# Encoder block on one core: eleven attention tiles are transposed in 32-by-32 blocks by VectorE and put in place by DMA, and six weight strips get their low halves from GpSimd

## The reference, cut to what matters

```python
def axial_gqa_attention(q, k, v, q_g, k_g):
    q = rms_norm(q.reshape(bsz, seq, A_Q_HEADS, HEAD_DIM), q_g)
    k = rms_norm(k.reshape(bsz, seq, A_KV_HEADS, HEAD_DIM), k_g)
    ...
    def block(s0):
        qb = lax.dynamic_slice_in_dim(q, s0, Q_BLOCK, axis=1)
        s = jnp.einsum('bqkgd,bskd->bkgqs', qb, k).astype(jnp.float32)
        p = jax.nn.softmax(s, axis=-1).astype(v.dtype)
        return jnp.einsum('bkgqs,bskd->bqkgd', p, v)
```

## Time and profile before

| what | us |
|---|---|
| median of 3 runs | 862.43 (862.28 to 864.42) |
| the profiled execution | 861.86 |
| its span in the profile | 859.8 |
| TensorE busy in the span | 839.4 (98%) |
| VectorE busy | 379.3 (44%) |
| ScalarE busy | 264.1 (31%) |
| GpSimd busy | 29.0 (3%) |

### The profile page before, as it was taken

One profiled execution on the slowest core, in us unless ns is written; L12 is line 12 of the kernel. 1 busy time (PEld: TensorE's weight loads), 2 busy tenths in 40 slices (PEclk: granted clock), 3 DMA queues, 4 the chain that ended last, 5 costly groups with the idle time before them and its releaser, 6 DMA issues.

```text
span 859.8 us, 10399 instructions
## 1 busy us (share of the span) xinstructions
PE 839.4 (98%) x4197; PEld 513.2 (60%) x4197; DVE 379.3 (44%) x665; ACT 264.1 (31%) x461; POOL 29.0 (3%) x50
## 2 busy tenths in 40 slices
PE   9999999999999999999999999999999998989996
PEld 8898866687878888888534343344433433334343
DVE  6377987797715254427322237223131321321351
ACT  6333876695624233216011010010100101001231
POOL 1050000000000000003000000000000000000010
PEclk9999999999999999999999999999999999999999
DMA  9830112023034234884899999999999999999996
GB/s 285 179 98 2 50 50 98 25 76 109 20 123 143 84 107 144 311 356 180 331 410 425 429 428 426 429 428 427 428 428 427 426 430 428 426 423 429 427 420 265
DMA packets 81490, 239.19 MB, mean 278 GB/s; under 512 B 8102, under 2 KB 63526, under 8 KB 65828
## 3 DMA queue, kind: packets, MB, share of 16 engines
q1 hardware_dynamic: 76016, 235.94, 69.7%
q10 hardware_dynamic: 5284, 2.09, 1.0%
q0 software_dynamic: 144, 0.51, 0.1%
HBM read 235.92 MB, written 2.62 MB: 277 GB/s over the span
## 4 chain that ended last, share of the span: by engine, by line
PE 88%; DMA 8%; DVE 1%; ACT 1%; issue 1%; POOLq 0%; POOL 0%; SPq 0%; DVEq 0%; ACTq 0%
PE psum L1657 21%; PE psum L1169 11%; PE psum L1689 11%; PE psum L1171 11%; PE psum L1170 11%; DMA wslot<-in_w_down 7%; PE psum L1614 3%; PE psum L1708 3%; PE psum L1357 2%; PE psum L1818 2%; PE psum L1326 2%; PE psum L1369 1%; PE psum L1669 1%; PE psum L1175 1%; PE psum L1622 1%; PE psum L1379 1%
## 5 line engine op out<-in xcount | busy, mean ns | idle before, releaser
L1657 PE MATMUL psum<-wslot,xinT 128*64 128x512 f32 x1000 | 221.9, 595 | 3.7 <-DMA wslot<-in_w_up 1.9
L1657 PEld LDWEIGHTS psum<-wslot,xinT 128*64 128x64 f32 x1000 | 69.5, 137 | 141.3 <-issue 131.8
L1689 PE MATMUL psum<-wslot,actT 128*64 128x512 f32 x424 | 95.8, 596 | 4.5 <-DMA wslot<-in_w_down 4.5
L1169 PE MATMUL psum<-hT_hi,w_hi 128*128 128x512 f32 x208 | 82.4, 396 | 0.9 <-DVE oT_lo L1991 0.9
L1170 PE MATMUL psum<-hT_lo,w_hi 128*128 128x512 f32 x208 | 81.2, 390 | 0.0
L1171 PE MATMUL psum<-hT_hi,w_lo 128*128 128x512 f32 x208 | 81.2, 390 | 0.0
L1892 DVE TENSOR_TENSOR w_lo<-w_raw,w_hi 128x1024 fp32r<-128x1024 f32 (+1 forms) x46 | 52.9, 1174 | 44.4 <-ACT w_hi L805 44.3
L1689 PEld LDWEIGHTS psum<-wslot,actT 128*64 128x64 f32 x424 | 29.4, 137 | 60.4 <-issue 58.0
L1101 ACT ACTIVATE actT<-psum 128x512 f32<-128x512 f32 x16 | 9.6, 597 | 171.2 <-PE psum L1669 171.2
L2305 DVE TENSOR_TENSOR x<-x,psum 128x512 f32<-128x512 f32 x48 | 29.7, 681 | 57.0 <-PE psum L1708 57.0
L2295 DVE TENSOR_TENSOR y_lo<-psum,y_hi 64x512 fp32r<-64x512 f32 x28 | 19.3, 689 | 80.4 <-ACT y_hi L1111 80.0
(11 more groups left out here) (285 smaller groups left out, 1306.5 us busy)
## 6 DMA issues: line engine op xcount, KB each, us to landing
wslot<-in_w_up SPq DMA_DIRECT2D x24, 2048.0 KB, 25.0
wslot<-in_w_gate SPq DMA_DIRECT2D x24, 2048.0 KB, 23.9
wslot<-in_w_down SPq DMA_DIRECT2D x22, 2048.0 KB, 22.4
w_raw<-in_w_in SPq DMA_DIRECT2D x34, 512.0 KB, 4.7
wslot<-in_w_up SPq DMA_DIRECT2D x15, 1024.0 KB, 11.0
wslot<-in_w_down SPq DMA_DIRECT2D x15, 1024.0 KB, 27.5
wslot<-in_w_gate SPq DMA_DIRECT2D x14, 1024.0 KB, 11.2
w_raw<-in_w_out SPq DMA_DIRECT2D x8, 512.0 KB, 4.9
```

Source lines behind the costliest of these rows:

```text
L1169: pe.matmul(out_, s_hi, m_hi, start=(k == 0), stop=False)
L1657: mm = pe.matmul(bank[2 * e + n][CAP * f:CAP * f + CAP, :], xinT[:, HALF * h + k, CAP * e:CAP * e + CAP], wslot[place_of(m)][:, k % PART, ...
L1689: mm = pe.matmul(bank[4 + e][CAP * f:CAP * f + CAP, :], actT[:, e, k, CAP * h:CAP * h + CAP], wslot[place_of(m)][:, k % PART, SEQ * f:SEQ ...
```

## The change

In the even heads (0, 2, 4, 6) the tiles 0, 1 and 2 (in head 6 only 0 and 1) no longer go over TensorE: eleven tiles of 32. For those the steps are:

- VectorE only makes the reciprocal; ScalarE multiplies the tile (`scale_probs`), ahead of which TensorE's transposes, and after which `read_probs`, are gone.
- VectorE transposes all 32x32 blocks of the tile with one instruction into a new buffer `blocks` (`turn_blocks`), one unit after the reciprocal.
- SP copies `blocks` into `pT` with 16 DMAs of 32 partitions for each of the four heads (`move_blocks`), ahead of the loads of strips 18, 21, 23 and 24.
- `pT` and `oT` get another order of tokens, which ScalarE and VectorE undo when they read the result of `values_a`. `values_a` now also waits for `blocks_in` and stands in units 10, 18 and 26.

The low halves of strips 14 to 19 move from VectorE to GpSimd. The `far` copy of mixer B moves from ahead of its first unit to ahead of its second.

The core of the diff:

```diff
+        def block_tiles(h):
+            return NT - 2 if h == A_HEADS - 2 else NT - 1
+        def in_blocks(u):
+            return u < NA and u // NT % 2 == 0 and u % NT < block_tiles(u // NT)
...
-        O_READ, O_LOW = (10, 19, 26), (11, 21, NA)
-        A_LOWS = (5, 7, 10, 16, 20, 26)
+        MOVES_BEHIND = (18, 21, 23, 24)
+        VALUES_AT = (10, 18, 26)
+        O_READ, O_LOW = (11, 20, 27), (12, 22, NA)
+        POOL_SPLITS = range(14, 20)
...
+            def move_blocks(h):
+                sp.wait_ge(blocks_turned, blocks_before(NT * h + NT))
+                if h >= 2:
+                    sp.wait_ge(pv_done, h // 2)
+                for kq in range(NT):
+                    for q in range(NT):
+                        sp.dma_start(pT[SQ * kq:SQ * kq + SQ, 0, :, P * q:P * q + SQ * block_tiles(h)],
+                                     blocks[SQ * q:SQ * q + SQ, :, kq, 0:SQ * block_tiles(h)]).then_inc(blocks_in, 16)
...
+            for n in POOL_SPLITS:
+                pool.wait_ge(w_split, n)
+                pool.wait_ge(w_hi_done, n + 1)
+                raw, hi, lo = parts_of(n)
+                pool.tensor_tensor(lo, raw, hi.bitcast(F32), ALU.subtract).then_inc(w_split, 1)
...
+            def scale_probs(u):
+                act_.wait_ge(probs_normed, u + 1)
+                p = probs_of(u)[:, 0:SEQ]
+                act_.activation(p, p, ACT.Copy, scale=column(rinv, u)).then_inc(probs_scaled, 1)
...
             def turn_probs(u):
+                if in_blocks(u):
+                    return
                 pe.wait_ge(probs_normed, u + 1)
...
             def norm_probs(u, width):
                 dve.wait_ge(exp_done, u + 1)
+                if in_blocks(u):
+                    dve.reciprocal(column(rinv, u), column(rsum, u)).then_inc(probs_normed, 1)
+                    return
...
+            def turn_blocks(u):
+                head, c = divmod(u, NT)
+                if c == 0 and head >= 2:
+                    wait_blocks_in(dve, head - 2)
+                dve.wait_ge(probs_scaled, blocks_before(u + 1))
+                dve.transpose(blocks[:, :, :, SQ * c:SQ * c + SQ].rearrange("p k q s -> p (k q) s"),
+                              probs_of(u)[:, 0:SEQ].rearrange("p (b s) -> p b s", s=SQ)).then_inc(blocks_turned, 1)
...
-                if u in A_LOWS:
-                    split_lo(14 + A_LOWS.index(u))
...
-            settle(dve.tensor_copy(far[:, :], dist[:, 0, SEQ:SEQ + 2 * P]))
...
+                        if u == NA + 1:
+                            settle(dve.tensor_copy(far[:, :], dist[:, NT - 1, SEQ:SEQ + 2 * P]))
```

More of the change, by code:

```diff
@@ L56 @@
 KIB = 1024
+SQ = 32
 COL_A = 0
@@ L392, in probs_of, with whole_before, blocks_before, wait_blocks_in @@
             return (probs_a if u < NA else probs_b)[u % 3]
+        def block_tiles(h):
+            return NT - 2 if h == A_HEADS - 2 else NT - 1
+        def in_blocks(u):
+            return u < NA and u // NT % 2 == 0 and u % NT < block_tiles(u // NT)
+        def whole_before(u):
+            return sum(not in_blocks(v) for v in range(u))
+        def blocks_before(u):
+            return u - whole_before(u)
+        def wait_blocks_in(eng, h):
+            eng.wait_ge(blocks_in, 16 * NT * NT * (h // 2 + 1))
         def wait_probs_free(eng, u):
             before = u - 3 if u < NA else max(u - 3, NA - 1)
-            if before >= 0:
-                eng.wait_ge(probs_turned, before + 1)
+            if before >= 0 and in_blocks(before):
+                eng.wait_ge(blocks_turned, blocks_before(before + 1))
+            elif before >= 0:
+                eng.wait_ge(probs_turned, whole_before(before + 1))
+        def turned_bank(u):
+            return tp[(0, 3)[whole_before(u) % 2]]
+        def token_order(i, rows):
+            if i >= OA:
+                return rows
+            return rows.rearrange("p (q c s) -> p c q s", q=NT, c=NT)
+        def by_tiles(i, rows):
+            if i >= OA:
+                return rows
+            return rows.rearrange("p (c q s) -> p c q s", q=NT, c=NT)
         def column(of, u):
@@ L930, in _ @@
                     if u == 3 * NA // 4:
-                        act_.dma_start(dist[:, :, :], distance).then_inc(dist_in, 16)
-                if 2 <= u < NA + 2:
+                        act_.dma_start(dist[:, :, :], distance).then_inc(shape_parts_in, 16)
+                if u and in_blocks(u - 1):
+                    scale_probs(u - 1)
+                if 2 <= u < NA + 2 and not in_blocks(u - 2):
                     read_probs(u - 2)
@@ L1398, in _ @@
                     scores_a(u + 2)
-                if u > 1 and u % (2 * NT) == 1:
-                    values_a(u // (2 * NT) - 1)
+                if u in VALUES_AT:
+                    values_a(VALUES_AT.index(u))
                 fill(A_FILL, u, cols_a, A_LEAD)
@@ L2018, in _ @@
                     norm_probs(u - 1, SEQ)
+                if u >= 2 and in_blocks(u - 2):
+                    turn_blocks(u - 2)
                 for g in range(N_COL_A):
```

51 lines of the change are left out of this document (32 added, 19 removed).

## The result

The changed kernel takes 869.76 us (median of 4 runs, 868.48 to 871.0) against 862.38 before: ratio 1.0077, 95% interval 1.0061 to 1.0094. It is slower, where I had forecast 1.0 us faster. A second set of runs of the same kernel gave 866.74 us (865.78 to 868.64) against 863.14, ratio 1.0054 [1.0037, 1.0071]. The profiled execution of the first set took 869.02 us, span 867.2.

The account below looks back on a forecast made before the run. TensorE was taken to bound mixer A. Eight tiles x 0.45 less 2.8 for the first head, less 0.1 for strips, plus 0.3 for `far`: 1.0 us faster, 861.4 us, range 857.8 to 864.5.

Parts of the forecast that it names:

- TensorE bounds mixer A; a tile in blocks takes 0.45 us off it: Mixer A: TensorE has no idle time, so each tile's dropped transposes save 0.45 us, 4.9 us for eleven tiles.
- The first head, GpSimd's hold: Mixer A's units 3 and 4: GpSimd's low halves hold off VectorE's multiplications, so TensorE turns unit 4 2.8 us late.
- No hold: Rival, first head: GpSimd and VectorE run together without waiting; 3.6 us faster, 858.8 us; chance 0.32.
- GpSimd goes twice: Rival, first head: strip 16 starts before unit 3's waiting multiplication, unit 4 4.7 us late; 863.3 us; 0.14 with slow block transposes.
- Strips 17 to 19 cost 0.1 us: Later in mixer A: GpSimd's low halves of these strips delay multiplications, costing TensorE 0.1 us, at most 1.5.
- Moves: 16 x 0.42 + 2.8 = 9.5 us for a head: Block moves: sixteen issues 0.42 us apart plus 2.8 us landing; head 6 has 10.8 us, so 1.3 us are left.
- Heads 2 and 4 start when the `values_a` before ends and are needed 14 us or more later.: Moves of heads 2 and 4: 14 us or more available against 9.5 us for a head's moves.
- blocks come late: Rival: slower issues make TensorE wait for moved blocks at head 6 and head 0; 865 us and more, to 868; chance 0.08.
- The `far` copy, 0.3 us: Start of mixer B: the copy stands 0.33 us ahead of the first masked maximum; moving it gains 0.3 us.

Follow-up runs that it names:

- two_heads: three_heads with the last head also whole, so six tiles in blocks and no moves beside the distance load; 861.21 us, ratio 0.9980 to the kernel before.
- dist_late: Changed kernel with only the distance table's load issued four units later, in unit 28 instead of 24; 863.96 us.
- pool_only: Kernel before with only the six low halves moved from VectorE to GpSimd, no blocks; 868.73 us.
- three_25: three_heads with the distance load issued at unit 25 instead of 28; 4.4 us of mixer A's length for this one number.
- pause: Kernel before with four additions put ahead of VectorE's multiplication of unit 15; a 3.44 us wait costs 5.24 us of mixer A's length.
- lows_dist: Changed kernel with the six low halves back on VectorE and the distance load issued four units later; no gain shows, last `values_a` waited 1.99 us.
- three_heads: lows_dist with head 0 whole and one tile of the last head in blocks, seven tiles in all; 861.32 us, ratio 0.9983 to the kernel before.
- far_only: Kernel before with only the `far` copy moved behind mixer B's first unit; TensorE idle there 0.62 us for 0.93, nothing shows in the time.

## Why the prediction was wrong, step by step

- **TensorE bounds mixer A; a tile in blocks takes 0.45 us off it.** Right. For two_heads 76.43 - 6 x 0.45 + 1.43 = 75.16, measured 75.12; for dist_late 77.04 against 77.05. That these two come so near is in part luck, as the other kernels are off by up to 0.4.
- **The first head, GpSimd's hold.** Right in mechanism and nearly in size. Counted from the start of mixer A, which came 2.84 us late in that profile, unit 3's multiplication ended at 97.28 (forecast 97.95), unit 4's at 100.92 (101.35), and TensorE turned unit 4 at 100.98 (101.4): 2.4 us late for 2.8. The rule of the Trainium skill (SBUF — State Buffer, "Who interferes with whom") agrees with the trace: the multiplication ends 0.28 us behind GpSimd's instruction each time. A low half took 2.46 us for my 2.9, a block transpose 0.70 for 0.65. "No hold", my second case with 0.32, fell. "GpSimd goes twice" wasn't seen.
- **Strips 17 to 19 cost 0.1 us.** Right in this kernel: the multiplication at 126.02 took 1.74 us and TensorE didn't wait. pool_only shows my upper bound of 1.5 too low: there one strip (at 137.88, the last) cost a wait of 2.17 us and the low clock behind it. My reason, that TensorE turns a tile some 1.1 to 1.5 us after it is ready, doesn't hold for the whole mixer. In the trace before, the multiplication and the transposes of one tile (DVE, PE):

```profile
137.75 0.49 DVE L1987 TENSOR_SCALAR probs_a<-probs_a,small 128x512 f32<-128x512 f32 x1
```

```profile
138.31 0.64 PE L1357 MATMUL psum<-ident,probs_a 128*128 128x128 f32 x4
```

Here TensorE turns it 0.07 us after it is ready. That no such tile was hit in the changed kernel is in part luck.
- **Moves: 16 x 0.42 + 2.8 = 9.5 us for a head.** This term was mis-sized. I took the issue of a 128 KB load for that of a move; it takes 0.65 us as a rule, whether the move is of 48, 32 or 16 KB, and a move lands after 2.0 when alone. From the first issue to the last landing there are fifteen steps, not sixteen: 15 x 0.65 + 2.0 = 11.75 us. I had named 0.50 us as the point from which TensorE waits for head 6. TensorE was ready for it 10.4 us behind the first issue (170.15 - 159.73; my 10.8), so it should wait 1.3; it waits 1.26.
- **"Heads 2 and 4 start when the `values_a` before ends and are needed 14 us or more later."** This is the step that failed. Head 4's moves don't start at the end of the second `values_a` (135.62) but when VectorE has turned unit 18 (136.82 + 0.70), at 137.55; TensorE is ready for them at 150.69, 13.1 us later. 1.4 us were left, not 4.5. I gave the rival "blocks come late" the place head 6 and head 0 and left out this head. That rival, with a chance of 0.08, came nearest in time (867.8), but 3.93 of the 5.19 us of waits are at a head that it doesn't name.
- **The distance load.** It stands in no step of mine at all, though it moved 1.5 MB in the same stretch of the trace before (issued at 143.86, landed after 6.3 us). I asked which queues the moves pass, and not whose transfers share the DMA engines with them. It turned 1.4 us of slack into 3.93 of wait: dist_late leaves 0.42 of it, where a single issue of head 4 took 1.77 us, and three_25 brings it back.
- **The clock.** The sum had only waits in it. Behind the 3.93 us the granted clock fell to half, 1.4 us more, and pause shows it without the change. In pool_only it is 1.5 us.
- **The `far` copy, 0.3 us.** Seen as idle time, not in the medians.

The sum in its terms, against the forecast 1.0 faster: -4.95 tiles, +3.44 first head, +3.93 head 4, +1.26 head 6, +1.39 clock, which is 5.1 us more; the length shows 4.74. The 0.33 between them lie behind the third `values_a`: from the fill step after it to the last `values_a`, without the wait, the changed kernel takes 10.57 us and dist_late 10.87. A stop ahead of one tile's transposes, 0.13 us before and 0.29 in dist_late, isn't there. That the pause has let the other engines get ahead is argued, not shown. The start of mixer B gains 1.10 us (5.09 us from the last `values_a` to the next fill, 6.19 before). Of that 0.3 are the `far` copy, my only term for it; the rest is the other side of the 1.26 us wait, by the 0.77 that two_heads showed. So the net is 3.64 us. In the second set the mixer starts 0.26 later, and 0.26 + 3.69 = 3.95 stand against 3.92 between the profiled executions (865.78 - 861.86). In the first, 2.84 from the opening and 3.64 make 6.48 of 7.16; the other 0.7 lie behind, and I haven't placed them.

## What to carry to other kernels

A transfer that takes the place of work on the bounding engine has three prices: the issue times of all its pieces (measure them for the shape at hand; here 0.65 us each whatever the size, and single ones up to 1.77), the landing, and whatever else the DMA engines carry in that window, from any queue. Write down for every consumer when its last piece starts and when it is wanted; one number that moves a big load by a few units was worth 4 us of this stage here. Measure a stage to a point at which every engine's backlog has been used up: a wait just ahead of the end can be one that would have come right behind it. And price a wait of the bounding engine above its length: what follows a pause can run at the lower clock.

## What the hardware showed that I had not expected

- TensorE at half clock behind a pause: after 3.44 us (pause), 3.93 (after), 2.17 (pool_only), 1.99 (lows_dist), with 1.4 to 1.8 us lost each time. The waits of 1.62 and 1.82 us in the first head and of 1.92 in three_heads were followed by the full clock.
- The start of the program in two forms: four matmuls in 1.98 to 2.34 us or in 3.78, with mixer A 2.3 to 2.9 us later. Three of the nine profiles of kernels with tiles in blocks have the late form: after, dist_late and two_heads (their mixer A began at 90.24, 90.00 and 90.01), so two_heads was not helped by it. None of the four of before, pool_only, far_only and pause has it. Whether the kernel before has it in some executions is therefore not shown, and what decides it stays open.
- A small SBUF-to-SBUF move that had landed after 2.0 us landed after up to 7.3 beside a 1.5 MB load on another queue.
- The issue of such a move, 0.60 us in the median, took 1.77 once in dist_late, 1.50 in three_heads and 1.22 in three_25, each time while 16 KB of instructions were being loaded.
